# Sparse attention: probabilities scaled on ScalarE, turned a job later, compressed keys' probabilities in their own place

## The reference, cut to what matters

```python
def masked_softmax(s, mask):
    s = jnp.where(mask, s.astype(F32), -jnp.inf)
    m = jnp.max(s, axis=-1, keepdims=True)
    e = jnp.exp(s - m)
    return e / jnp.maximum(jnp.sum(e, axis=-1, keepdims=True), 1e-30)
...
o_c = p_c @ vc; o_s = p_s @ v_g; o_w = p_w @ vwb
return gb[..., 0:1] * o_c + gb[..., 1:2] * o_s + gb[..., 2:3] * o_w
```

## Time and profile before

| | us |
|---|---|
| median of 3 runs | 2017.01 (2015.54 to 2018.52) |
| profiled execution | 2016.81 |
| its span, first to last instruction | 2015.0 |
| TensorE busy in the span | 1887.5 |
| VectorE busy | 803.5 |
| ScalarE busy | 663.2 |
| GpSimd busy | 542.4 |
| mean granted clock of TensorE | 0.972 |

### The profile page before, as it was taken

One profiled execution on the slowest core, in us unless ns is written; L12 is line 12 of the kernel. 1 busy time (PEld: TensorE's weight loads), 2 busy tenths in 40 slices (PEclk: granted clock), 3 DMA queues, 4 the chain that ended last, 5 costly groups with the idle time before them and its releaser, 6 DMA issues. The chain is left out here.

```text
span 2015.0 us, 28970 instructions
## 1 busy us (share of the span) xinstructions
PE 1887.5 (94%) x11709; PEld 1389.1 (69%) x11709; DVE 803.5 (40%) x1639; ACT 663.2 (33%) x1380; POOL 542.4 (27%) x420
## 2 busy tenths in 40 slices
PE   6999989998999989999999998999979999999997
PEld 4788977878788666677787876988765444444443
DVE  4467462254332355532524146143242343343333
ACT  4542233222224344446245246444332111111110
POOL 2342233225553333248145321253300000000000
PEclk9999999999899989899999999999989999999999
DMA  5230122123123212143132221232157999999994
GB/s 159 63 88 24 43 73 63 42 63 122 36 63 106 63 33 63 32 164 97 50 123 84 85 97 40 65 105 84 43 215 315 419 411 414 419 418 419 420 419 178
DMA packets 133209, 313.40 MB, mean 156 GB/s; under 512 B 15296, under 2 KB 103120, under 8 KB 108496
## 3 DMA queue, kind: packets, MB, share of 16 engines
q1 hardware_dynamic: 133072, 311.49, 41.5%
HBM read 309.37 MB, written 2.10 MB: 155 GB/s over the span
## 5 line engine op out<-in xcount | busy, mean ns | idle before, releaser
L321 POOL TENSOR_TENSOR unit_low<-unit_ring,unit_high 128x512 fp32r<-128x512 f32 x332 | 436.5, 1340 | 796.1 <-ACT unit_high L314 796.1
L358 PE MATMUL dense<-hT,unit_high 128*128 128x512 f32 x592 | 243.8, 412 | 3.0 <-DVE dense_temps L528 1.7
L359 PE MATMUL dense<-hT,unit_high 128*128 128x512 f32 x592 | 234.1, 395 | 0.0
L360 PE MATMUL dense<-hT,unit_low 128*128 128x512 f32 x592 | 233.9, 395 | 0.0
L314 ACT CAST unit_high<-unit_ring 128x512 fp32r<-128x512 f32 x332 | 185.9, 619 | 57.3 <-PE dense L360 28.2
L451 PE MATMUL dense<-unit_high,hT 128*128 128x256 f32 x704 | 203.7, 289 | 0.7 <-POOL unit_low L321 0.4
L452 PE MATMUL dense<-unit_low,hT 128*128 128x256 f32 x704 | 199.7, 284 | 0.0
L453 PE MATMUL dense<-unit_high,hT 128*128 128x256 f32 x704 | 199.7, 284 | 0.0
L451 PEld LDWEIGHTS dense<-unit_high,hT 128*128 128x128 f32 x704 | 135.5, 193 | 8.0 <-issue 2.6
L452 PEld LDWEIGHTS dense<-unit_low,hT 128*128 128x128 f32 x704 | 135.5, 192 | 0.6 <-issue 0.5
L453 PEld LDWEIGHTS dense<-unit_high,hT 128*128 128x128 f32 x704 | 135.4, 192 | 0.0
(11 more groups left out here) (590 smaller groups left out, 3472.5 us busy)
## 6 DMA issues: line engine op xcount, KB each, us to landing
expert_ring<-w_exp_gate SPq DMA_DIRECT2D x64, 1024.0 KB, 9.6
expert_ring<-w_exp_up SPq DMA_DIRECT2D x64, 1024.0 KB, 10.5
expert_ring<-w_exp_down SPq DMA_DIRECT2D x64, 1024.0 KB, 9.0
unit_ring<-w_in SPq DMA_DIRECT2D x55, 1024.0 KB, 5.3
unit_ring<-w_br SPq DMA_DIRECT2D x16, 512.0 KB, 6.4
unit_ring<-w_mkv SPq DMA_DIRECT2D x8, 1024.0 KB, 5.4
x<-x SPq DMA_DIRECT2D x8, 512.0 KB, 5.7
w_out_raw<-w_out SPq DMA_DIRECT2D x4, 1024.0 KB, 10.2
```

Of the source, the lines that this page charges most:

```text
L321: nc.gpsimd.tensor_tensor(low[:, at:at + 512], raw[:, at:at + 512], high[:, at:at + 512], ALU.subtract).then_inc(*self.split.up())
L358: nc.tensor.matmul(out, high[:, k, c], rh, start=(k == 0), stop=False)
L359: nc.tensor.matmul(out, high[:, k, c], rl, start=False, stop=False)
L360: last = nc.tensor.matmul(out, low[:, k, c], rh, start=False, stop=(k == kd - 1))
```

## The change

`scale` is split. A new `weigh(j)` on VectorE clamps and inverts the row sums as before and multiplies them by the gates, two columns in one instruction. `scale(j)` is now on ScalarE: two multiplications in place by that factor, one per head. In step j VectorE gets the maxima of j and weigh(j - 1); ScalarE gets the exponentials of j, scale(j - 1), keep(j - 3); TensorE gets scores(j), turn(j - 3), mix(j - 4). The loop is one step longer. The probabilities of the compressed jobs (31 columns) have two places in a tile of their own, `few`; those of the other jobs go round in the three places of `pr`. An exponential waits for the turn of the job whose place it takes: j - 6 (compressed), j - 5 (selected), j - 4 (window). The list of dense steps is the same.

```diff
-    pr = place("probs", 60 * KB, [P, 3, 2, SEQ])
+    pr, few = place("probs", 60 * KB, [P, 3, 2, SEQ]), place("few_probs", 33 * KB + 128, [P, 2, 2, 32])
...
+    def probs(j, i):
+        g, b = j // 3, j % 3
+        return pr[:, (2 * g + b - 1) % 3, i, 0:jobs[j]["n"]] if b else few[:, g % 2, i, 0:N_CMP]
+
+    def before(j):
+        g, b = j // 3, j % 3
+        at = 2 * g + b - 4
+        return at // 2 * 3 + at % 2 + 1 if b else j - 6
...
-            if j >= 3:
-                act.wait_ge(*turn_token[first_fill[j - 2] - 1])
+            if before(j) >= 0:
+                act.wait_ge(*turn_token[first_fill[before(j) + 1] - 1])
...
-    def scale(j, dve):
+    def weigh(j, dve):
         job = jobs[j]
-        at = slice(2 * (j % 4), 2 * (j % 4) + 2)
+        f = inv[:, 2 * (j % 4):2 * (j % 4) + 2]
         dve.wait_ge(*exp_token[j, 1])
...
+        nc.vector.tensor_scalar(f, sums[:, 2 * (j % 4):2 * (j % 4) + 2], 1e-30, None, ALU.max).then_inc(*weighed.up())
+        dve.wait_ge(*weighed.now())
+        nc.vector.reciprocal(f, f).then_inc(*weighed.up())
+        dve.wait_ge(*weighed.now())
+        gate = gates[:, job["t"], :].rearrange("p (g h b) -> p g h b", g=2, h=4)[:, :, job["h"], job["b"]]
+        nc.vector.tensor_tensor(f, f, gate, ALU.mult).then_inc(*weighed.up())
+        weigh_token[j] = weighed.now()
+
+    def scale(j, act):
+        act.wait_ge(*weigh_token[j])
         for i in range(2):
-            p = pr[:, j % 3, i, 0:job["n"]]
-            gate = 3 * (4 * i + job["h"]) + job["b"]
-            last = nc.vector.tensor_scalar(p, p, inv[:, at.start + i:at.start + i + 1], gates[:, job["t"], gate:gate + 1], ALU.mult, ALU.mult)
+            p, at = probs(j, i), 2 * (j % 4) + i
+            last = nc.scalar.mul(p, p, inv[:, at:at + 1])
...
-    for j in range(n + 3):
+    for j in range(n + 4):
...
-            if 2 <= j < n + 2:
-                turn(j - 2, pe)
             if 3 <= j < n + 3:
-                mix(j - 3, pe)
+                turn(j - 3, pe)
+            if 4 <= j < n + 4:
+                mix(j - 4, pe)
...
-                scale(j - 1, dve)
+                weigh(j - 1, dve)
...
-            if 2 <= j < n + 2:
-                keep(j - 2, act)
-        if j >= 3 and (j - 3) % 12 == 11:
-            gate_by_z((j - 3) // 12)
+            if 1 <= j < n + 1:
+                scale(j - 1, act)
+            if 3 <= j < n + 3:
+                keep(j - 3, act)
+        if j >= 4 and (j - 4) % 12 == 11:
+            gate_by_z((j - 4) // 12)
```

More of the change, by code:

```diff
@@ L1874, in nsa_attention @@
     section = core.section
-    scored, maxed, exped, scaled, transposed, turned, mixed, gated = (core.sig(f"att_{n}") for n in (
-        "scored", "maxed", "exped", "scaled", "transposed", "turned", "mixed", "gated"))
+    scored, maxed, exped, weighed, scaled, transposed, turned, mixed, gated = (core.sig(f"att_{n}") for n in (
+        "scored", "maxed", "exped", "weighed", "scaled", "transposed", "turned", "mixed", "gated"))
     tabled = core.sig("att_table")
     sc = place("biased", 52 * KB, [P, 2, 2, SEQ])
-    pr = place("probs", 60 * KB, [P, 3, 2, SEQ])
+    pr, few = place("probs", 60 * KB, [P, 3, 2, SEQ]), place("few_probs", 33 * KB + 128, [P, 2, 2, 32])
     prT = place("probsT", 72 * KB, [P, 4, SEQ])
@@ L1904, in nsa_attention @@
     chunks = [-(-job["n"] // P) for job in jobs]
-    max_token, exp_token, scale_token, turn_token, keep_token, mix_token, table_token, gate_token = {}, {}, {}, {}, {}, {}, {}, {}
+    max_token, exp_token, weigh_token, scale_token, turn_token, keep_token, mix_token, table_token, gate_token = ({} for _ in range(9))
     fills = [[(0, 1)] if job["n"] <= 2 * P else [(0,), (1,)] for job in jobs]
@@ L1961, in exponentials @@
             act.wait_ge(*max_token[j, i])
-            if j >= 3:
-                act.wait_ge(*turn_token[first_fill[j - 2] - 1])
+            if before(j) >= 0:
+                act.wait_ge(*turn_token[first_fill[before(j) + 1] - 1])
             at = 2 * (j % 4) + i
-            nc.scalar.activation(pr[:, j % 3, i, 0:w], sc[:, j % 2, i, 0:w], ACT.Exp, bias=neg[:, at:at + 1], scale=-1.0,
+            nc.scalar.activation(probs(j, i), sc[:, j % 2, i, 0:w], ACT.Exp, bias=neg[:, at:at + 1], scale=-1.0,
                                  accum_out=sums[:, at:at + 1]).then_inc(*exped.up())
             exp_token[j, i] = exped.now()
-    def scale(j, dve):
+    def weigh(j, dve):
         job = jobs[j]
-        at = slice(2 * (j % 4), 2 * (j % 4) + 2)
+        f = inv[:, 2 * (j % 4):2 * (j % 4) + 2]
         dve.wait_ge(*exp_token[j, 1])
[L1973 to L1976, removed]
+        nc.vector.tensor_scalar(f, sums[:, 2 * (j % 4):2 * (j % 4) + 2], 1e-30, None, ALU.max).then_inc(*weighed.up())
[7 more added lines that the diff above has]
+        act.wait_ge(*weigh_token[j])
         for i in range(2):
-            p = pr[:, j % 3, i, 0:job["n"]]
-            gate = 3 * (4 * i + job["h"]) + job["b"]
-            last = nc.vector.tensor_scalar(p, p, inv[:, at.start + i:at.start + i + 1], gates[:, job["t"], gate:gate + 1], ALU.mult, ALU.mult)
+            p, at = probs(j, i), 2 * (j % 4) + i
+            last = nc.scalar.mul(p, p, inv[:, at:at + 1])
         last.then_inc(*scaled.up())
@@ L1994, in turn @@
                     w = min(P, jobs[j]["n"] - k * P)
-                    last = nc.tensor.transpose(t_bank[f % 2][0:w, at + k * P:at + (k + 1) * P], pr[:, j % 3, i, k * P:k * P + w], core.ident)
+                    last = nc.tensor.transpose(t_bank[f % 2][0:w, at + k * P:at + (k + 1) * P], probs(j, i)[:, k * P:k * P + w], core.ident)
             last.then_inc(*transposed.up())
```

## The result

The change makes the kernel slower: 2022.65 us median (2014.12 to 2025.44, 20 runs) against 2016.16 (2006.99 to 2019.59, 20 runs), ratio 1.0037, 95% interval 1.0026 to 1.0049. A second comparison gave 1.0051 (1.0030 to 1.0071). The forecast was "no change", 2016 us.

What follows compares the result with a forecast made beforehand. The sparse stage was taken as bound by TensorE plus its stalls. Stalls +1.5 us and clock -2.7 us gave -1.2 from 2016.81, 2015.6; with the median 0.2 higher, 2015.8, rounded 2016 us; range 2001 to 2027, 8 in 10.

Steps and rivals of the forecast that it cites:

- The stalls of before: Sparse stage: 12 TensorE waits for VectorE's scaling, 16.9 us, all in the step behind one without dense work.
- The chain that is late next: Scores, first maximum, two exponentials, two multiplications, copy: new TensorE stalls of 18.4 us in place of the 16.9 us.
- ScalarE's cost: The 96 added multiplications take 36.8 us back to back; ScalarE goes from 101 to about 138 of 213 us.
- The factor, 0.6 us of three links: weigh on VectorE: three links of 0.17 us, 0.6 us in all; bounds 0.4 and, where GpSimd works, 2.8 us.
- The maxima's waits, 2.8 us: TensorE's 7 waits for the row maxima in the sparse stage would stay at 2.8 us.
- The clock, -2.7 us: TensorE's granted clock in the sparse stage: six slow stretches for seven, 2.7 us each, so -2.7 us.
- Own place: Compressed keys' probabilities stored separately: exponentials wait for an older turn, already done; nothing either way.
- gate_by_z: Runs a step later; its 0.69 us of VectorE falls beside scores in all four heads.
- the drain: One more step at the loop's end: step 51 holds only mix(47), 1.1 us previously in step 50; 0.1 us.
- The sum: Whole kernel: +1.5 us stalls and -2.7 us clock give -1.2 us against the profiled execution; forecast 2016 us, chance 0.38.
- Rival B: ScalarE becomes the bound in steps 9, 12, 24, 42: 4.5 us plus two slow stretches, 5.4; 2026 us, chance 0.23.
- Rival A: The waits really go, multiplications filling ScalarE's gaps: 1984 us, halfway about 2002; chance 0.29, a third for the whole.

Runs made afterwards that it cites:

- The other list of dense steps: Kernel before with steps without dense work moved to every third and 9, 21, 33 (31 dense steps for 30): 1987.73 us, ratio 0.9893.
- the own place alone: Kernel before with only the compressed keys' probabilities in a place of their own: 2010.81 us, ratio 1.0000 to before.
- Copies first: Changed kernel with keep(j - 3) ahead of scale(j - 1) in ScalarE's queue, nothing else: 1987.43 us, ratio 0.9879 to the kernel before.
- Two instructions instead of three: Changed kernel with gates inverted once beforehand, so weigh is one clamp-and-multiply and one reciprocal: 2014.38 us, ratio 1.0007 to the kernel before.

## Why the prediction was wrong, point by point

- **The stalls of before**: right. The other list of dense steps removed them, the own place alone left them.
- **The chain that is late next**: right in kind and, for the long stalls, in place. Each of the seven steps that I had as long (12, 17, 24, 29, 32, 44, 47) stalls on the copy, with 2.01, 1.96, 2.34, 1.53, 2.25, 1.59 and 2.91 us where I had 2.2, 2.1, 2.0, 1.9, 2.2, 1.65 and 2.4: 14.6 us for 14.5. Copies first shows that it is the scale pair in front of the copy.
- **ScalarE's cost**: right, 135 us busy in the stage for 138. The multiplications took 0.712 us at 512 columns (0.715 taken) and 0.305 at 31 (0.313):

```profile
L1997 ACT ACTIVATE probs<-probs,inverse 128x512 f32<-128x512 f32 x16 | 10.6, 712 | 2.4 <-DVE inverse L1990 2.4
...
L1997 ACT ACTIVATE few_probs<-few_probs,inverse 128x31 f32<-128x31 f32 x30 | 7.8, 305 | 1.1 <-DVE inverse L1990 1.1
```

- **The factor, 0.6 us of three links: the step that failed.** The term was mis-sized. I had the delay by GpSimd as a bound (up to 2.8 us) and put it into few steps (12, 17 and 24). The rows, against the earlier trace rows:

```profile
L1985 DVE TENSOR_SCALAR inverse<-row_sums 128x2 f32<-128x2 f32 x47 | 15.8, 337 | 0.0
L1990 DVE TENSOR_TENSOR inverse<-inverse,gates 128x2 f32<-128x2 f32 x47 | 15.3, 325 | 1.6
...
L1987 DVE RECIPROCAL inverse<-inverse 128x2 f32<-128x2 f32 x47 | 7.8, 166 | 1.6
```

  The new product takes 0.325 us on average and not 0.17, since it is held up too, and the reciprocal between the two never is; so the products are 15.3 us and not 8, and VectorE lost 26 us of work instead of 31. Of L1985 14 of 48 take over 0.3 us, of L1990 10 of 48. All 24 run beside a GpSimd instruction, and 22 of them end 0.02 to 0.03 us behind one; 13 reciprocals ran beside GpSimd too and none was held. Step 37, where I had 0.3 to 0.6 us of stall and 1.70 were measured:

```profile
823.84 3.75 POOL L321 TENSOR_TENSOR unit_low<-unit_ring,unit_high 128x512 fp32r<-128x512 f32 x3 [10.16 <-ACT unit_high L314]
...
826.62 0.98 DVE L1990 TENSOR_TENSOR inverse<-inverse,gates 128x2 f32<-128x2 f32 x1
...
827.64 0.53 ACT L1997 ACTIVATE few_probs<-few_probs,inverse 128x31 f32<-128x31 f32 x2 [1.10 <-DVE inverse L1990]
...
828.08 1.05 ACT L2022 COPY probsT<-core 128x512 f32<-128x512 f32 x2
...
828.78 0.41 PE L2012 MATMUL core<-ident,probs 128*128 128x128 f32 x2 [1.70 <-ACT probsT L2022]
```

  The product ends when GpSimd's subtractions do, the multiplication and the copy behind it start that much later. Steps 14 (1.09 for 0.3 to 0.6), 27 (0.59 for 0), 39 (0.97 for 0) and 42 (0.95 for 0.3 to 0.6) exceed the forecast as well, and at all four ScalarE waits for the factor too (0.69, 0.86, 0.94 and 0.49 us at 14, 27, 39 and 42), with L1985 or L1990 held beside GpSimd (L1985 1.05 us at 14 and 1.24 at 39, L1990 0.99 at 27 and 0.98 at 42). Together the probsT waits are 22.6 us for 18.4, and these five steps are nearly all of the difference. Two instructions instead of three gave 7.1 us back. The page that I cited, "VectorE: DVE Perf Modes" of the Trainium skill (section "Two Vector instructions with no wait between them"), says that an operation with two SBUF tensor inputs reads the second through an interface shared with GpSimd; the trace agrees (0.98 us for two columns), and I had priced it for steps 12 and 24 only. L1985 has one tensor input and is held no less.
- **The maxima's waits, 2.8 us**: 3.9, a further 1.1.
- **The clock, -2.7 us: not borne out**, and that is the second term that failed. In the stage it was better than I said: six stretches for seven and shorter, 0.95 against 0.91 and 0.93 in the two profiles of before. They lie behind steps 12, 17, 24, 29, 32 and 37, so 44 and 47 left none although I had them: six is right in number only. Over the runs the clock loss did not fall (54.8 against 51.9). In the profiles the stage's gain, 5 to 9 us, is given back behind it, where the code is the same. From 890 to 1450 us the changed kernel has four slow stretches where before has one, first after, then before:

```profile
890.00:1450.00 560.00, 533.66 (x3313) 444.62 (x3312) 201.94 (x374) 244.05 (x488) 217.77 (x165) 0.99 0.26 84
```
```profile
890.00:1450.00 560.00, 533.84 (x3331) 446.46 (x3330) 204.65 (x376) 246.03 (x492) 220.03 (x167) 1.00 0.27 89
```

  Summed over windows of 10 us that is a loss of 6.8 us of full clock against 1.7. Where the experts begin, 1450 to 1560 us, it is 13.7 against 10.3; of that the window of 1490 to 1520, in the same order:

```profile
1490.00:1520.00 30.00, 22.19 (x119) 22.00 (x119) 17.86 (x47) 10.45 (x12) 0.00 (x0) 0.56 0.99 413
```
```profile
1490.00:1520.00 30.00, 17.91 (x130) 17.54 (x128) 17.83 (x47) 11.50 (x13) 0.00 (x0) 0.72 1.01 423
```

  The second profiles of both kernels repeat these numbers. Ahead of the stage, in the same code again, the loss was 17.0 us in both profiles of after and 25.6 and 22.2 in those of before. So the profiled execution of the changed kernel, at 2016.31 us, came within a microsecond of my 2015.6 by luck. What makes these stretches come and go is open, and no profile shows one of the longer executions of the changed kernel.
- **Own place, gate_by_z, the drain**: right, nothing. The own place has a run of its own; for the other two the trace of the changed kernel shows no wait of TensorE behind step 47's.
- **The sum**: -1.2 us forecast. The full-clock part gave +6.5 where I had +1.5 for the stalls, and the clock +2.9 +- 2.0 where I had -2.7. Rival B, "ScalarE the bound" with 4.5 us more stalls, had the size but not the cause: with the same load and the copies first ScalarE bounds nothing. Rival A was wrong for this change; its 1984 us is near what a one-place move of `keep` makes of it (1987).

## What to carry to other kernels

When work is moved to an engine with time to spare, look at what is queued behind it there, not at the engine's load: put first what another engine waits for, and last what has a step of slack. Moving one call past another was worth 35 us of 2022 here, more than twice the wait that the change was about, since nearly half of it is clock that comes back with the stalls gone. And where stalls recur in a fixed rhythm, compare the rhythm of the filler work with that of the jobs before moving work between engines; a different list alone gave 1.1%, where the change with the copies first gave 1.2%.

## What the hardware showed beside it

A stall's length alone does not decide over the clock. In the changed kernel step 29's stall of 1.53 us is in a window with the clock at 0.72, while step 47's of 2.91 us, the longest, leaves it at 1.00. Nor does the step decide: the stall of step 17 in the kernel before, 1.56 and 1.55 us in its two profiles, is followed by 0.72 in the first and by 1.00 in the second. The two windows of the changed kernel:

```profile
791.00:797.00 6.00, 5.28 (x18) 3.83 (x20) 0.16 (x1) 2.24 (x9) 0.00 (x0) 0.72 0.52 171
...
872.00:878.00 6.00, 5.61 (x40) 4.33 (x41) 0.69 (x1) 3.03 (x7) 0.54 (x1) 1.00 0.06 5
```

A VectorE instruction on two columns can take 1.2 us when GpSimd works (L1973 and L1985 up to 1.24, L1990 up to 1.02, against 0.16 to 0.17 undisturbed), and a reciprocal on the same two columns took 165 to 167 ns each time, beside GpSimd or not.
